# Second norm taken bank by bank with its squares summed on the tensor engine, and gate2 made beside the first feed-forward chunk

## The reference, cut to what matters

```
mod = silu(c) @ w_ada + b_ada
shift1, scale1, gate1, shift2, scale2, gate2 = split(mod, 6)
h  = rmsnorm(x, norm_mix_g) * (1 + scale1) + shift1
proj = h @ w_in                        # -> attention heads, mLSTM heads
...
x  = x + gate1 * (concat(attn_out, mlstm_out) @ w_out)
h2 = rmsnorm(x, norm_mlp_g) * (1 + scale2) + shift2
x  = x + gate2 * (square(relu(h2 @ w_ff1)) @ w_ff2)
rmsnorm(x, g) = x * rsqrt(mean(x * x) + 1e-6) * g
```

## Time and profile before

| | |
|---|---|
| time, median of 3 runs | 2557.8 us (2556.95 to 2558.32) |
| span of the profiled execution | 2562.6 us, 4.8 over that median; no other time of that execution is given |
| tensor engine, matmul | 2346.7 us busy |
| tensor engine, weight load | 1928.8 us busy |
| vector engine | 956.8 us busy |
| ScalarE | 706.4 us busy |
| GpSimd | 922.6 us busy |
| mean granted clock of the tensor engine | 0.948 of full |

### The profile page before, as it was taken

How to read it: one execution, slowest core, us unless ns; L and a number is a source line. 1 busy time by engine, 2 the same in 40 slices (tenths; PEclk the granted TensorE clock), 3 DMA queues, 4 the chain that set the end, 5 groups by cost and what they waited for, 6 DMA issues and landing times.

```text
span 2562.6 us, 28381 instructions
## 1 busy us (share of the span) xinstructions
PE 2346.7 (92%) x10352; PEld 1928.8 (75%) x10352; DVE 956.8 (37%) x1380; ACT 706.4 (28%) x972; POOL 922.6 (36%) x438
## 2 busy tenths in 40 slices
PE   3679999986887787969999999999999999999999
PEld 3568788874665666858888888888888888888887
DVE  5868755505656547975111102111111011021111
ACT  3123333232334521224212213122122122131221
POOL 1014444421111123434444444444444444444442
PEclk7789999996888898989999999999999999999999
DMA  8876767620103538862233332332333322333332
GB/s 288 287 269 209 242 222 247 241 86 21 40 22 121 231 134 292 275 209 88 94 98 98 98 92 96 98 98 95 94 98 98 98 92 97 98 98 95 95 115 74
DMA packets 180064, 355.27 MB, mean 139 GB/s; under 512 B 13210, under 2 KB 23964, under 8 KB 179104
## 3 DMA queue, kind: packets, MB, share of 16 engines
q1 hardware_dynamic: 171216, 331.34, 39.4%
q10 hardware_dynamic: 8784, 23.07, 2.3%
HBM read 327.09 MB, written 27.28 MB: 138 GB/s over the span
## 4 chain that ended last, share of the span: by engine, by line
PE 74%; DVE 10%; DMA 6%; issue 6%; ACT 1%; POOL 1%; SPq 1%; DVEq 0%; ACTq 0%; POOLq 0%
PE ps L621 24%; PE ps L622 23%; PE ps L623 23%; DMA araw<-in_w_ada 5%; DVE acc L1417 4%; PE ps L655 1%; DVE yc L1588 1%; DVE acc L1414 1%; DMA gb<-g_d 1%; DVE sqacc L1878 0%; DVE pT L1725 0%; DVE stl L1598 0%; DVE pr L1718 0%; DMA wraw<-in_w_in 0%; POOL gbm L596 0%
## 5 line engine op out<-in xcount | busy, mean ns | idle before, releaser
L313 POOL TENSOR_TENSOR wlo<-wraw,whi 128x1024 fp32r<-128x1024 f32 (+2 forms) x372 | 888.4, 2393 | 1277.3 <-ACT whi L308 1269.2
L308 ACT ACTIVATE whi<-wraw 128x1024 fp32r<-128x1024 f32 (+2 forms) x376 | 390.6, 1045 | 1316.9 <-PE ps L623 1157.5
L621 PE MATMUL ps<-h2T,whi 128*128 128x512 f32 x1024 | 399.5, 390 | 3.1 <-DVE h2T L1900 3.1
L622 PE MATMUL ps<-h2T,whi 128*128 128x512 f32 x1024 | 399.1, 390 | 0.0
L623 PE MATMUL ps<-h2T,wlo 128*128 128x512 f32 x1024 | 399.1, 390 | 0.0
L621 PE MATMUL ps<-ah,whi 128*128 128x512 f32 x1024 | 398.6, 389 | 0.0
L623 PE MATMUL ps<-ah,wlo 128*128 128x512 f32 x1024 | 398.4, 389 | 0.0
L622 PE MATMUL ps<-al,whi 128*128 128x512 f32 x1024 | 398.3, 389 | 0.0
L1417 DVE SCALAR_TENSOR_TENSOR acc<-araw,silc,acc 128x512 f32<-128x512 f32 x360 | 330.3, 978 | 50.1 <-DMA araw<-in_w_ada 49.7
L1920 DVE TENSOR_TENSOR sq<-utmp 128x512 f32<-128x512 f32 x64 | 71.9, 1143 | 608.7 <-ACT utmp L1355 605.4
L1934 DVE SCALAR_TENSOR_TENSOR x1T<-ps,M,x1T 128x512 f32<-128x512 f32 x128 | 87.3, 745 | 548.1 <-PE ps L623 548.1
(11 more groups left out here) (264 smaller groups left out, 2539.4 us busy)
## 6 DMA issues: line engine op xcount, KB each, us to landing
wraw<-in_w_ff SPq DMA_DIRECT2D x256, 512.0 KB, 3.6
araw<-in_w_ada SPq DMA_DIRECT2D x192, 512.0 KB, 5.2
wraw<-in_w_in SPq DMA_DIRECT2D x72, 512.0 KB, 5.4
wraw<-in_w_out SPq DMA_DIRECT2D x32, 512.0 KB, 7.3
xnat<-in_x ACTq DMA_DIRECT2D x4, 1024.0 KB, 7.2
xT_d<-xT ACTq DMA_DIRECT2D x1, 4096.0 KB, 13.7
qk_d<-sth ACTq DMA_DIRECT2D x16, 256.0 KB, 3.0
qk_d<-stl ACTq DMA_DIRECT2D x16, 256.0 KB, 4.7
```

Source lines behind the costliest of these rows:

```text
L308: act.activation(whi[:, slot, 0:kb, 0:cols], wraw[:, slot, 0:kb, 0:cols], ACT.Copy).then_inc(hi_ready, 1)
L313: pool.tensor_tensor(wlo[:, slot, 0:kb, 0:cols], wraw[:, slot, 0:kb, 0:cols], whi[:, slot, 0:kb, 0:cols].bitcast(F), ALU.subtract).then_in ...
L621: pe.matmul(dst, lhs[0], rhs[0], start=start, stop=False)
L622: pe.matmul(dst, lhs[0], rhs[1], start=False, stop=False)
```

## The change

The last block of group 3 is run bank by bank (`last_out_block`), and each finished bank is handed to the vector engine by a semaphore of its own (`o_bank`). The last four squares get four buffers and are not added up; the tensor engine sums five arrays (the running sum of groups 0 to 2 and the four squares) in the accumulators. The scaling reads the broadcast row from bank 5, without the copy by ScalarE. Pairs 8 and 9 only are made beside the out-projection, with six, eight and two units ahead of the residuals of groups 0, 1 and 2.

```diff
@@ -179,9 +179,9 @@
         x1T = at(st, "x1T", [P, KT, S])
-        with ExitStack() as s2:
-            araw2 = at(s2, "araw2", [P, 4, 2, 512])
         ah0 = at(st, "ah", [P, CT, S], R)
+        araw2 = at(st, "araw2", [P, 4, 2, 512])
+        acc2 = at(st, "acc2", [P, 4, 512])
     mixst.close()
@@ -200,8 +200,6 @@
     with ExitStack() as st:
-        with ExitStack() as s2:
-            acc2 = at(s2, "acc2", [P, 4, 512])
         al0 = at(st, "al", [P, CT, S], R)
@@ -267,6 +265,7 @@
                                                sem("x1_done"), sem("o_sq"), sem("o_sqadd"))
+    o_bank = sem("o_bank")
     u2_done, h2_hi, h2_lo = sem("u2_done"), sem("h2_hi"), sem("h2_lo")
@@ -476,34 +475,45 @@
-        def out_units(pair, us):
-            for u in us:
-                later_ada_load(pair, u, araw2)
+        def late_unit(i):
+            for w in range(2):
+                later_ada_load(8 + i // 8, 2 * (i % 8) + w, araw2)
         for b in range(3, 7):
...
         sp.wait_ge(xT_stored, 16)
-        out_units(8, range(4))
+        late_unit(0)
+        late_unit(1)
         out_load(0, 7)
-        out_units(8, range(4, 8))
+        late_unit(2)
+        late_unit(3)
         sp.dma_start(x1T[:, :, :], xT_d).then_inc(xT_back, 16)
-        with sp.Fori(1, G_OUT) as g:
+        for g in range(1, G_OUT):
             for b in range(GB):
                 out_load(g, b)
-                out_units(7 + g if b < 4 else 8 + g, [(2 * b + 8) % 16, (2 * b + 9) % 16])
-        out_units(11, range(8, 16))
-        def ff1_loads(ch):
+                if 4 + GB * (g - 1) + b < 16:
+                    late_unit(4 + GB * (g - 1) + b)
+        def gate2_unit(s):
+            if s in (6, 7):
+                late_unit(16 + s - 6)
+            elif 9 <= s <= 22:
+                late_unit(16 + s - 7)
+        def ff1_loads(ch, beside=lambda s: None):
             for q in range(2):
...
                                w_ff13[:, KB * b:KB * b + KB, bass.ds(CH * ch + 512 * q, 512)])
-        def ff2_loads(ch, q):
+                    beside(GB * q + b)
+        def ff2_loads(ch, q, beside=lambda s: None):
             for b in range(CT // KB):
...
                            w_ff23[:, bass.ds(CT * ch + KB * b, KB), 512 * q:512 * q + 512])
+                beside(2 * GB + 4 * q + b)
@@ -512,7 +522,10 @@
             sp.dma_start(out3[:, :, c], yst[:, :, c]).then_inc(y_stored, 16)
-        with sp.Fori(0, CHUNKS - 1) as ch:
+        ff1_loads(0, gate2_unit)
+        for q in range(4):
+            ff2_loads(0, q, gate2_unit)
+        with sp.Fori(1, CHUNKS - 1) as ch:
             ff1_loads(ch)
@@ -901,31 +914,46 @@
-        def out_pair(gp, start=0):
-            for h in range(2):
-                g = 2 * gp + h
-                if not (h == 0 and start):
-                    pe.wait_ge(o_free[h], 4 * gp + 4)
-                    pe.wait_ge(ada_read, 2 * (7 + g))
-                for b in range(GB):
-                    if h == 0 and b < start:
-                        continue
-                    if b == 4 and not (isinstance(g, int) and g == 0):
-                        pe.wait_ge(o_free[1 - h], 4 * gp + 4 + 4 * h)
-                        ada_sum(7 + g, acc2[:, 2 * (1 - h):2 * (1 - h) + 2, :], 4 * (1 - h) + 3)
+        def out_group(g, start=0):
+            h = g % 2
+            if g >= 1:
+                pe.wait_ge(o_free[h], 4 * (g // 2) + 4)
+            if g == 3:
+                pe.wait_ge(ada_read, 18)
+            for b in range(start, GB):
+                if b == 4 and g >= 2:
+                    pe.wait_ge(o_free[1 - h], 4 * (g // 2) + 4 + 4 * h)
+                    ada_sum(6 + g, acc2[:, 2 * h:2 * h + 2, :], 4 * (1 - h) + 3)
+                if g == 3 and b == GB - 1:
+                    last_out_block()
+                else:
                     group_block(N_OUT + GB * g + b, b, h, mix, GB, False)
+        def last_out_block():
+            pe.wait_ge(lo_ready, N_OUT + GB * G_OUT)
+            for m in range(4):
+                for k in range(KB):
+                    kt = KT - KB + k
+                    ins = passes(ps[:, 4 + m, :], wtile(3, k, m * P, (m + 1) * P),
+                                 [mix(i, kt) for i in range(2)], False, k == KB - 1)
+                ins.then_inc(o_bank if m < 3 else blk_done, 1)
         pe.wait_ge(m_olo, 2 * HM)
-        out_pair(0, 3)
-        with pe.Fori(1, G_OUT // 2) as gp:
-            out_pair(gp)
-        pe.wait_ge(o_sqadd, KT + 1)
+        out_group(0, 3)
+        for g in range(1, G_OUT):
+            out_group(g)
         pe.wait_ge(o_free[0], 12)
-        ada_sum(11, acc2[:, 2:4, :], 3)
-        norm_sum(pe, n2, 0, [sqacc2[:, :]])
-        norm_bcast(pe, n2, 1, utmp2[:, 1, :])
-        pe.wait_ge(o_free[1], 12)
-        pe.wait_ge(n2[5], 1)
-        pe.wait_ge(ada_read, 24)
+        pe.wait_ge(ada_read, 20)
+        for i, sq in enumerate((sqacc2[:, :], sq2[:, 0, :], sq2[:, 1, :], utmp2[:, 0, :], utmp2[:, 1, :])):
+            if i == 0:
+                pe.wait_ge(o_sqadd, 13)
+            else:
+                pe.wait_ge(o_sq, 12 + i)
+            for t in range(TT):
+                ins = pe.matmul(ps[:, t, 0:1], sq[:, t * P:(t + 1) * P], ones[:, 0:1],
+                                start=(i == 0), stop=(i == 4))
+        ins.then_inc(n2[0], 1)
+        norm_bcast(pe, n2, 5, utmp2[:, 1, :])
@@ -937,18 +965,28 @@
-        def ff_chunk(ch, last=False):
+        def ff_chunk(ch, first=False, last=False):
             for q in range(2):
                 pe.wait_ge(f_free[q], 12 * ch + 4)
+                if first and q == 1:
+                    pe.wait_ge(o_free[1], 12)
                 for b in range(GB):
+                    if first and q == 1 and b == 6:
+                        pe.wait_ge(f_free[0], 8)
+                        ada_sum(10, acc2[:, 0:2, :], 3)
                     group_block(N_FF + CB * ch + GB * q + b, b, q, lambda i, kt: h2T[i][:, kt, :], GB, False,
...
                 pe.wait_ge(f_free[q % 2], 12 * ch + 4 * (q // 2 + 2))
+                if first and q in (0, 2):
+                    pe.wait_ge(ada_read, 22 + q)
                 if last and q >= 2:
...
                 for b in range(CT // KB):
+                    if first and q == 1 and b == 3:
+                        pe.wait_ge(f_free[0], 12)
+                        ada_sum(11, acc2[:, 2:4, :], 3)
                     group_block(N_FF + CB * ch + 2 * GB + 4 * q + b, b, q % 2,
@@ -956,7 +994,8 @@
                 y_transposes(3)
-        with pe.Fori(0, CHUNKS - 1) as ch:
+        ff_chunk(0, first=True)
+        with pe.Fori(1, CHUNKS - 1) as ch:
             ff_chunk(ch)
@@ -1316,9 +1355,8 @@
             act.wait_ge(x1_done, T + 1)
-            act.wait_ge(o_sqadd, T)
-            act.activation(sq2[:, i % 2, :], x1T[:, T, :], ACT.Square).then_inc(o_sq, 1)
-        norm_scale(act, n2, 1, rstd2[:, :])
+            act.wait_ge(o_sqadd, 13)
+            act.activation((sq2, utmp2)[i // 2][:, i % 2, :], x1T[:, T, :], ACT.Square).then_inc(o_sq, 1)
@@ -1854,24 +1892,34 @@
-        def residual(gp, half):
-            g = 2 * gp + half
-            units = lambda us: ada_units(8 + g, us, araw2, acc2[:, 2 * half:2 * half + 2, :], False)
-            units(range(4))
-            if not (isinstance(g, int) and g == 0):
-                m = M_G1 + 8 * (3 + g)
-                ada_cols(7 + g, 4 * (1 - half) + 3, m, m + 4)
-            units(range(4, 8))
-            if isinstance(g, int) and g == 0:
+        def late_units(i0, i1):
+            for i in range(i0, i1):
+                pair = 8 + i // 8
+                ada_units(pair, [i % 8], araw2, acc2[:, 2 * (pair % 2):2 * (pair % 2) + 2, :], False)
+        def residual(g):
+            half = g % 2
+            late_units((0, 6, 14, 16)[g], (6, 14, 16, 16)[g])
+            if g >= 2:
+                m = M_G1 + 8 * (2 + g)
+                ada_cols(6 + g, 4 * (1 - half) + 3, m, m + 4)
+            if g == 0:
                 dve.wait_ge(xT_back, 16)
-            dve.wait_ge(blk_done, N_OUT + GB * g + GB)
+            if g == 3:
+                dve.wait_ge(ada_read, 20)
+                link(dve.scalar_tensor_tensor(A1[:, :], M[:, M_SC2:M_SC2 + KT], 1.0,
+                                              VT[:, V_GMLP:V_GMLP + KT], ALU.add, ALU.mult))
             for i in range(4):
                 T = 4 * g + i
-                dve.scalar_tensor_tensor(one(x1T, T), ps[:, 4 * half + i, :], col(M, M_G1 + T), one(x1T, T),
+                if g == 3 and i < 3:
+                    dve.wait_ge(o_bank, i + 1)
+                else:
+                    dve.wait_ge(blk_done, N_OUT + GB * g + GB)
+                dve.scalar_tensor_tensor(x1T[:, T, :], ps[:, 4 * half + i, :], col(M, M_G1 + T), x1T[:, T, :],
                                          ALU.mult, ALU.add).then_inc(x1_done, 1)
...
             dve.sem_inc(o_free[half], 4)
-            for i in range(4):
+            for i in range(4 if g < 3 else 0):
                 T = 4 * g + i
```

(33 more changed lines are left out.)

## The result

The changed kernel takes 2572.49 us (median of 4 runs, 2571.48 to 2574.78) beside 2558.06 us for the kernel before on the same chip (4 runs, 2556.95 to 2560.49): ratio 1.0051, 95% interval [1.0038, 1.0064]. It is slower by 13 us by the ratio (14.4 between the medians); the prediction was 2541.5 us, 16.3 faster, and its range ended at 2552.

The account below looks back on a forecast made before the run. The tensor engine was taken as the bound, pausing at 998 us and in the hand-over for late vector, ScalarE and SyncE work. Terms: -5.8 - 1.8 - 15.9 + 3.7 + 3.5 = -16.3 us, giving 2541.5 us, range 2532 to 2552.

Parts of the forecast that it names:

- part 4: gate2 in the first feed-forward chunk: two column sums give back 3.7 us, waits 3.5 us (bounds 0 and 10).
- (e): Slower rival: SyncE's queue in the first feed-forward chunk serialised, at 8 us a unit 33 us: 2571 us; chance 0.05.
- Rival (c): SyncE's queue in the first feed-forward chunk holds more, 6 us plus 2 for the clock: 2549.5 us; chance 0.12.
- the priced waits: First feed-forward chunk: 2.0 us at block 14's column sum, 1.5 us at block 20, both under 4.3 us.
- Parts 1 and 2: Out-projection: earlier residual of group 0 wins 5.8 us (bounds 0 to 8.3); one column sum fewer wins 1.8 us.
- what is late next: Out-projection group 1: loads of blocks 5 to 7 stand behind conditioning loads, block 7 late; 2.5 us charged.
- Rival (b): The hole at 998, ahead of group 1's block 3, stays because DMA engines are the limit: 2547.3 us; chance 0.13.
- Part 3: Hand-over from out-projection to feed-forward: 11.2 us instead of 27.1, 15.9 us won, the clock taken to fall.
- rival (a): Clock holds through the hand-over: broadcast 1.12 instead of 2.08 us, no cold start, 3.3 us better, 2538.2; chance 0.18.
- Rival (d): The new column sums in the hand-over run at half clock, 8.8 us instead of 4.6: 2545.7 us; chance 0.06.
- The scaling's price: Scaling with its row read from the accumulators: price nothing; some 2 us at three places come off the vector engine.
- Unrolled loops: Unrolled loops and the smaller descriptor area cost nothing; bounds 1 us either way.

Follow-up runs that it names:

- e1: The changed kernel with the read of pair 10's columns moved ahead of the second half's activation work: 2549.18 us, ratio 0.9956.
- e5: e1 with conditioning loads one weight block later from block 4 of group 1 on, so blocks 5 to 7 are asked for earlier: 2545.05 us, 0.9942.
- e2: The kernel before with the new second norm alone, gate2 staying beside the out-projection: 2555.12 us, ratio 0.9979.
- e4: e1 plus 18 full-size matmuls into unused bank 6 around the broadcast: 2549.68 us, ratio 0.9961.
- e11: e1 with five gate2 units (16 to 20) moved out of the first feed-forward chunk, behind group 2's residual: 2541.64 us, ratio 0.9926.
- e3: e1 with the old second norm, so gate2's move alone: 2558.54 us, ratio 0.9995.
- e9: e5 with eight gate2 units (16 to 23) moved from the first feed-forward chunk to around group 2's residual: 2546.31 us, ratio 0.9948.
- e7: e1 with the load order of e5, later column sums and loads in the first feed-forward chunk, and the fillers of e4: 2543.79 us, 0.9934.
- e10: e9 with the filling matmuls of e4: 2545.63 us, ratio 0.995.
- e12: The changed kernel run again unaltered, on the same chip as e11: 2570.43 us, ratio 1.0039.
- e8: e1 run again unaltered, on the chip of e5 and e7: 2545.32 us, ratio 0.9942.

## Why the prediction was wrong

**The step that failed: part 4.** It counted "32 loads, 64 vector steps, two column sums and their reads", priced the sums, loads and steps, and asked what they make late. Of the reads it said no more and so put them at nothing, without a reason, though they are what the tensor engine waits for by name before blocks 16 and 24. The step worked out that units 19 to 23 end at 32 to 37 us after block 8's start and that the second activation work is ahead of unit 26, and so had all that was needed: the read stands behind that activation work and four units more. The activation work of the second half can only begin when block 15 is done: 2.7 us behind the start of the last matmul (1226.42 - 1223.69); ScalarE has a weight split ahead of it at 1224.85 and starts the relu at 1225.81. It takes 7.4 us, and the four units 14.6 (to 1248.39). That is the pause, 24.55 us, and 2.2 us are lost to the half clock behind it (11.40 us at 0.81). The profile before could not show it, for there the reads stood beside the out-projection; the program order in the diff did. No rival named it either: (e), the slower one, was SyncE's queue in units 19 to 31, and the time it gave (2571) fits the result by chance alone. In e1 that queue cost 1.87 and 2.76 us at two places, not 33. Rival (c), which put 8 us more than the forecast on it, went too far as well: with the clock, e1 has 8.0 us there where the forecast had 3.5.

**Part 4, the priced waits.** Block 14: 1.82 us after, 1.87 in e1, where 2.0 was charged. Block 20: 2.76 in e1 for 1.5, bounds 0 to 4. What was wrong is to take from their being shorter than 4.3 us that such waits cost no clock. The windows view of e1 behind each:

```profile
1214.60:1224.60 10.00, 9.98 (x45) 8.42 (x46) 6.91 (x10) 2.12 (x2) 4.78 (x2) 0.83 0.94 319
1253.70:1263.70 10.00, 10.00 (x37) 8.10 (x38) 10.00 (x12) 2.12 (x2) 4.77 (x2) 0.83 0.85 285
```

A granted clock of 0.83 over 10 us is 3.4 us at half clock, 1.7 us lost, at each place. C of e1 adds up with it: 3.7 (two sums) + 1.87 + 2.76 + 3.4 = 11.7 us, measured 1420.2 - 1408.4 = 11.8. In the changed kernel: 3.7 + 1.82 + 1.7 + 24.55 + 2.2 = 34.0, measured 33.9. Part 4 said 7.2.

**Parts 1 and 2.** The residual of group 0 starts 9.2 us after A begins (985.44 - 976.22; 8.5 predicted), and the hole at 998 is gone. A is 6.4 us shorter where 7.6 were forecast. The price charged for "what is late next" was 2.5 us, at block 7; it is 3.81 at block 5 with a clock of 0.83 behind. The cause is the one given, and e5 shows it. In SyncE's queue after, the load of block 5, issued at 998.83, stands behind a conditioning load:

```profile
986.38 0.47 SPq L300 DMA_DIRECT2D wraw<-in_w_out  x1
997.76 1.03 SPq L377 DMA_DIRECT2D araw<-in_w_ada  x2
998.83 0.47 SPq L300 DMA_DIRECT2D wraw<-in_w_out  x1
```

Rival (b), that the hole stays, is out. e2, which leaves the units where they were, keeps a pause of 5.96 us there.

**Part 3** holds. 11.37 us measured, 11.2 forecast, and 11.36 to 13.4 in every kernel with both halves of the change. The sums at full clock, the scaling at its price and the feed-forward weights split in time came as written. The clock fell (0.71 in the stretch, 0.83 behind it), so rival (a) did not come. In e4, where the fillers hold the clock, the ten microseconds behind the hand-over are at 1.00 against 0.80 in e1, 2.0 us of work in one execution and nothing that the runs can tell. Rival (d), cold sums, came partly: the five sums take 4.5 us after and 6.6 in e11.

The scaling's price rested on its operand. In the earlier trace rows a scaling beside a split took 2.76 us. After, the one at 1136.55 with its row in the accumulators runs at 0.75 through a split that starts at 1136.19, and it is the low part behind it, with its operands in SBUF, that is held (vector engine's timeline after):

```profile
1136.55 0.75 DVE L1470 SCALAR_TENSOR_TENSOR utmp<-x1T,A,ps 128x512 f32<-128x512 f32 x1
1137.21 2.11 DVE L1943 SCALAR_TENSOR_TENSOR h2T<-utmp,M,h2T 128x512 fp32r<-128x512 f32 x1
```

In e3, where the row is in SBUF, the scaling at 1137.83 takes 2.77. This is the rule of the Trainium skill, SBUF — State Buffer, Who interferes with whom: a vector instruction with two SBUF inputs contends with a GpSimd instruction that reads SBUF, and one with at most one such input, outside the modes that use two ports, does not. The trace agrees, with 2.77 and 2.11 us against 0.75.

**Unrolled loops and the sum.** Unrolling shows no cost: C of e2, with the loop, is 1408.1, and e9's written-out chunk 1411.5 with 3.7 us of sums in it. Of the 27.7 us by which the three stretches miss the forecast (-16.3 forecast, +11.4 measured), 26.7 are part 4, 1.2 parts 1 and 2, -0.2 part 3. Without the misplaced read the kernel ran at 0.9942 to 0.9956, 11 to 15 us faster, where the forecast ratio was 0.9936.

## What to carry to other kernels

When work is moved to another stage, follow each semaphore that it ends in, the smallest reads included: list for every wait of the bottleneck engine which instruction releases it and what stands ahead of that instruction in its own engine's program, and put the end of that chain beside the time of the wait. A read of 0.22 us cost 25 us for standing behind the activation work and four units, though its engine had idled 10 us before. And a load that waits for a buffer, in an in-order queue, delays every load behind it: spreading work over idle stretches pays only where its loads don't stand ahead of the weights (e9 against e11, which also differ in how many units they spread, eight and five).

## What the runs showed of the hardware that was not expected

Short pauses of the tensor engine can cost clock, not always. The windows view over the 10 us behind each pause of the out-projection and the first chunk shows it. Behind the eight pauses of 1.24 to 1.67 us (e3 to e7 and e10) the granted clock was 1.00. Of the twenty of 1.74 to 4.00 us, sixteen had 0.66 to 0.86 behind them, such as 1.82 us after and 2.76 us in e1 (0.83 each), and four had 1.00. The same length can do either: 1.74 us had 0.83 in e12 and 1.00 in e8. Some of these pauses end in a column sum and others in full-size matmuls, and both kinds fell (1.88 us in e3, ahead of a weight block, 0.83). The windows view of two of the four at full clock, in e8, and then of the lowest, behind 2.44 us in e4:

```profile
1208.00:1218.00 10.00, 9.98 (x52) 8.61 (x53) 5.99 (x10) 2.12 (x2) 4.78 (x2) 1.00 0.93 318
1008.20:1018.20 10.00, 9.96 (x44) 8.22 (x45) 10.00 (x9) 3.19 (x3) 5.90 (x3) 1.00 0.98 345
...
1203.30:1213.30 10.00, 9.90 (x38) 8.63 (x39) 6.95 (x10) 2.12 (x2) 3.90 (x2) 0.66 0.92 324
```

A pause of 1.7 to 4 us in this kernel is thus to be priced at its length plus 0 to 3.4 us (0.34 of 10 us). And 18 full-size matmuls that nobody reads kept the clock at 0.91 and 0.92 through a hand-over in which it otherwise fell (e4), without a gain that could be measured.
